# Layer norm of a convolution branch: mean and variance as four 32-column matmuls and one ones-product

## The reference, cut to what matters

```python
def layer_norm(x, gain, bias):
    xf = x.astype(jnp.float32)
    mu = jnp.mean(xf, axis=-1, keepdims=True)
    xc = xf - mu
    y = xc * lax.rsqrt(jnp.mean(xc * xc, axis=-1, keepdims=True) + EPS)
    ...
def conv_module(val, gate, dw_kernel, dw_bias, ln_gain, ln_bias):
    u = val * jax.nn.sigmoid(gate)
    u = lax.conv_general_dilated(u, ...)   # causal, depthwise, width 31
    u = layer_norm(u, ln_gain, ln_bias)    # over 512 channels
    return jax.nn.silu(u)
```

## Time and profile before

| | |
|---|---|
| median of three runs | 1696.66 us |
| span of the profiled execution | 1691.3 us |
| PE busy | 1543.5 us (91%) |
| DVE busy | 1233.8 us (73%) |
| ACT busy | 873.8 us (52%) |
| the four means and four variances, TensorE records of L521 and L528 | 64, of some 0.6 us each |

### The profile page before, as it was taken

One profiled execution on the slowest core, in us unless ns is written; L12 is line 12 of the kernel. 1 busy time (PEld: TensorE's weight loads), 2 busy tenths in 40 slices (PEclk: granted clock), 3 DMA queues, 4 the chain that ended last, 5 costly groups with the idle time before them and its releaser, 6 DMA issues. The chain is left out here.

```text
span 1691.3 us, 23716 instructions
## 1 busy us (share of the span) xinstructions
PE 1543.5 (91%) x7340; PEld 1130.4 (67%) x7342; DVE 1233.8 (73%) x1950; ACT 873.8 (52%) x1529; POOL 367.2 (22%) x395
## 2 busy tenths in 40 slices
PE   2699989999999999999999999847999999999974
PEld 2588846688956788855889766525667767677641
DVE  4589776479885498875497973486688778887737
ACT  2322363423384423474324263246688778887746
POOL 1000000100001000001000011014466667665640
PEclk9999998999999999999999999859999999999997
DMA  9342343233322333332332453169999998789959
GB/s 333 120 149 78 123 156 143 75 100 100 89 99 88 100 100 100 113 100 75 88 99 77 182 156 99 74 241 326 357 299 286 325 290 247 201 247 283 276 114 381
DMA packets 200420, 291.25 MB, mean 172 GB/s; under 512 B 10558, under 2 KB 158171, under 8 KB 200346
## 3 DMA queue, kind: packets, MB, share of 16 engines
q1 hardware_dynamic: 170720, 197.15, 34.0%
q0 software_dynamic: 29360, 92.99, 20.0%
q10 hardware_dynamic: 266, 0.14, 0.0%
HBM read 240.42 MB, written 59.26 MB: 177 GB/s over the span
## 5 line engine op out<-in xcount | busy, mean ns | idle before, releaser
L979 DVE SCALAR_TENSOR_TENSOR cv<-late_rows,taps,cv 128x512 f32<-128x512 f32 x480 | 321.7, 744 | 0.1
L1896 DVE TENSOR_TENSOR w_rest<-wgu,w_high 128x1024 fp32r<-128x1024 f32 x192 | 233.8, 1221 | 89.8 <-ACT w_high L1819 86.4
L1819 ACT ACTIVATE w_high<-wgu 128x1024 fp32r x192 | 201.7, 1054 | 97.0 <-PE pgu L1764 73.3
L497 PE MATMUL bank<-wo,yT 128*128 128x512 f32 x512 | 224.2, 594 | 3.6 <-ACT hT L683 2.5
L468 PE MATMUL bank<-hT_high,tiles_operand 128*128 128x512 f32 x512 | 204.3, 399 | 9.6 <-DVE hT_operand L952 8.5
L469 PE MATMUL bank<-hT_operand,tiles_operand 128*128 128x512 f32 x512 | 203.6, 398 | 0.0
L470 PE MATMUL bank<-hT_high,win_operand 128*128 128x512 f32 x512 | 203.6, 398 | 0.0
L497 PEld LDWEIGHTS bank<-wo,yT 128*128 128x128 f32 x512 | 95.7, 190 | 118.3 <-issue 116.3
L1774 PE MATMUL py<-wd,hTe 128*128 x384 | 172.7, 592 | 1.8 <-DVE hTe L1919 0.9
L1762 PE MATMUL pgu<-w_high,x_high 128*128 128x512 f32 x384 | 156.2, 407 | 3.8 <-DVE x_rest L1911 3.8
L1763 PE MATMUL pgu<-w_rest,x_high 128*128 128x512 f32 x384 | 151.4, 394 | 0.0
(11 more groups left out here) (369 smaller groups left out, 2824.9 us busy)
## 6 DMA issues: line engine op xcount, KB each, us to landing
win<-w_in_in SPq DMA_DIRECT2D x64, 512.0 KB, 5.0
wgu<-w_gate_in SPq DMA_DIRECT2D x32, 1024.0 KB
wgu<-w_up_in SPq DMA_DIRECT2D x32, 1024.0 KB
wd<-w_down_in SPq DMA_DIRECT2D x32, 1024.0 KB
win<-w_in_in SPq DMA_DIRECT2D x16, 1024.0 KB, 5.1
wo<-w_ada_in POOLq DMA_DIRECT2D x6, 2048.0 KB, 9.5
y_dram<-zeros POOLq DMA_DIRECT2D x17, 512.0 KB, 5.7
tiles<-x_in POOLq DMA_DIRECT2D x16, 512.0 KB, 6.1
```

Of the source, the lines that this page charges most:

```text
L497: last = nc.tensor.matmul(out[:], yT[:, w % 2, k, :], wo[:, k, half * 512:(half + 1) * 512], start=(k == 0), stop=(k == KD - 1))
L979: ins = V.scalar_tensor_tensor(out=cv[:, j], in0=u[:, j, w:w + T], scalar=tap, in1=cv[:, j], op0=ALU.mult, op1=ALU.add)
L1819: A(w_high[:, QK * q:QK * q + QK, :], c.wgu[:, bass.ds(slot, 1), QK * q:QK * q + QK, :].rearrange("p a k n -> p (a k) n"), ACT.Copy).then_ ...
L1896: V.tensor_tensor(w_rest[:, part, :], c.wgu[:, bass.ds(slot, 1), part, :].rearrange("p a k n -> p (a k) n"), w_high[:, part, :].bitcast(F3 ...
```

## The change

The mean is formed in two steps. Four matmuls, one for each slab, multiply 32 columns of ones (not 128) and write each its own 32 partitions of `pS`; they don't accumulate over each other. VectorE copies `pS` to SBUF (`save_mean`, into a slab of `sq` that is free), and one more matmul with the full ones (`whole_mean`) sums over the partitions. Since every sum then stands 32 times, the scale of the mean is divided by `GROUP` = 32 more. The variance is done alike, but ScalarE makes the copy (`save_variance`). Four semaphores are added. Where the entries stand in the lists is changed as well: "mean2" and "var2" are the second products, "msave" and "vsave" the copies.

```diff
             def mean(t):
                 pe.wait_ge(conv_step, (t + 1) * CONV_STEPS)
                 wait(pe, masked, t * NT)
                 for k in range(NCH):
-                    last = nc.tensor.matmul(pS[:], c.ones[:], cv[:, k, :], start=(k == 0), stop=(k == NCH - 1))
-                last.then_inc(mean_ready, 1)
+                    nc.tensor.matmul(pS[k * GROUP:(k + 1) * GROUP, :], c.ones[:, 0:GROUP], cv[:, k, :],
+                                     start=True, stop=True).then_inc(mean_parts, 1)
+
+            def whole_mean(t):
+                pe.wait_ge(mean_saved, t + 1)
+                nc.tensor.matmul(pS[:], c.ones[:], sq[:, NCH - 1, :], start=True, stop=True).then_inc(mean_ready, 1)
 
             def variance(t):
                 wait(pe, o_saved, t * NT)
                 for k in range(NCH):
                     pe.wait_ge(squared, t * NCH + k + 1)
-                    last = nc.tensor.matmul(pO[:], c.ones[:], sq[:, k, :], start=(k == 0), stop=(k == NCH - 1))
-                last.then_inc(var_ready, 1)
+                    nc.tensor.matmul(pO[k * GROUP:(k + 1) * GROUP, :], c.ones[:, 0:GROUP], sq[:, k, :],
+                                     start=True, stop=True).then_inc(var_parts, 1)
+
+            def whole_variance(t):
+                pe.wait_ge(var_saved, t + 1)
+                nc.tensor.matmul(pO[:], c.ones[:], sq[:, 1, :], start=True, stop=True).then_inc(var_ready, 1)
...
+            def save_variance(t):
+                act.wait_ge(var_parts, (t + 1) * NCH)
+                A(sq[:, 1, :], pO[:], ACT.Copy).then_inc(var_saved, 1)
...
+            def save_mean(t):
+                dve.wait_ge(mean_parts, (t + 1) * NCH)
+                V.tensor_copy(sq[:, NCH - 1, :], pS[:]).then_inc(mean_saved, 1)
```

The heads of the lists, before and after. TensorE:

```diff
-            FIRST = [("mean",), ("ada", 0), ("ada", 1), ("T", 0), ("var",), ("A", 0), ("T", 1), ("B", 0), ...
+            FIRST = [("mean",), ("ada", 0), ("mean2",), ("ada", 1), ("T", 0), ("var",), ("T", 1), ("var2",), ("A", 0), ("B", 0), ...
-            MIDDLE = [("y", 0, 0), ("T", 0), ("mean",), ("T", 1), ("y", 0, 1), ("T", 2), ("var",), ("T", 3), ("y", 1, 0),
+            MIDDLE = [("y", 0, 0), ("mean",), ("T", 0), ("mean2",), ("T", 1), ("y", 0, 1), ("T", 2), ("var",), ("T", 3), ("var2",),
-            FINAL = [("y", 0, 0), ("mean",), ("y", 0, 1), ("var",), ("y", 1, 0), ("y", 1, 1), ("A", 0), ...
+            FINAL = [("y", 0, 0), ("mean",), ("y", 0, 1), ("mean2",), ("y", 1, 0), ("var",), ("y", 1, 1), ("var2",), ("A", 0), ...
```

More of the change, by code:

```diff
@@ L613, in bias_rows @@
                 taken[3] = mod_ready, 3
-            FIRST = [("mean",), ("ada", 0), ("ada", 1), ("T", 0), ("var",), ("A", 0), ("T", 1), ("B", 0), ("O", 0), ("T", 2),
+            FIRST = [("mean",), ("ada", 0), ("mean2",), ("ada", 1), ("T", 0), ("var",), ("T", 1), ("var2",), ("A", 0), ("B", 0), ("O", 0), ("T", 2),
                      ("A", 1), ("columns",), ("B", 1), ("T", 3), ("O", 1), ("A", 2), ("oT", 0), ("B", 2), ("rows",),
@@ L624, in _ @@
                      ("r", 3), ("oT", 2), ("oT", 3), ("l", 3), ("piece", 1)]
-            FINAL = [("y", 0, 0), ("mean",), ("y", 0, 1), ("var",), ("y", 1, 0), ("y", 1, 1), ("A", 0), ("B", 0), ("O", 0),
+            FINAL = [("y", 0, 0), ("mean",), ("y", 0, 1), ("mean2",), ("y", 1, 0), ("var",), ("y", 1, 1), ("var2",), ("A", 0), ("B", 0), ("O", 0),
                      ("r", 0), ("A", 1), ("B", 1), ("l", 0), ("O", 1), ("A", 2), ("oT", 0), ("r", 1), ("B", 2),
@@ L643, in steps @@
                     else:
-                        {"y": y_half, "r": router_turn, "l": logits, "mean": mean, "var": variance, "A": scores, "B": state_sums,
+                        {"y": y_half, "r": router_turn, "l": logits, "mean": mean, "mean2": whole_mean, "var": variance, "var2": whole_variance, "A": scores, "B": state_sums,
                          "O": outputs, "oT": turn_outputs}[kind](t, *at)
@@ L865, in _ @@
                      ("raw", 1), ("sq", 0), ("sq", 1), ("sq", 2), ("xsum", 3), ("sq", 3), ("raw", 2), ("exps", 1),
-                     ("end", 1), ("raw", 3), ("ln", 3), ("exps", 2), ("end", 2), ("var",), ("ysum", 0), ("exps", 3),
+                     ("end", 1), ("vsave",), ("raw", 3), ("ln", 3), ("exps", 2), ("end", 2), ("var",), ("ysum", 0), ("exps", 3),
                      ("end", 3), ("gate",), ("key", 0), ("x1sum", 0), ("ysum", 1), ("key", 1), ("rin", 0), ("osq", 0),
@@ L872, in _ @@
             FINAL = [("ln", 0), ("ln", 1), ("ln", 2), ("end", 0), ("exps", 0), ("sq", 0), ("sq", 1), ("sq", 2), ("sq", 3),
-                     ("exps", 1), ("end", 1), ("ln", 3), ("exps", 2), ("end", 2), ("var",), ("ysum", 0), ("exps", 3),
+                     ("exps", 1), ("vsave",), ("end", 1), ("ln", 3), ("exps", 2), ("end", 2), ("var",), ("ysum", 0), ("exps", 3),
                      ("end", 3), ("gate",), ("key", 0), ("x1sum", 0), ("ysum", 1), ("key", 1), ("rin", 0), ("osq", 0),
@@ L888, in steps @@
                     else:
-                        {"ln": log_forget, "exps": head_exps, "end": end_exp, "sq": squares, "var": variance, "gate": conv_gate,
+                        {"ln": log_forget, "exps": head_exps, "end": end_exp, "sq": squares, "vsave": save_variance, "var": variance, "gate": conv_gate,
                          "ysum": y_sums, "x1sum": x1_sums, "rin": router_in, "key": save_keys, "osq": square_outputs,
@@ L1080, in centre @@
                 for k in range(NCH):
[L1081 removed]
+                    V.scalar_tensor_tensor(out=cv[:, k], in0=pS[:], scalar=-1.0 / (GROUP * DC), in1=cv[:, k],
                                            op0=ALU.mult, op1=ALU.add).then_inc(centred, 1)
@@ L1135, in gate_outputs @@
                 last.then_inc(o_gated, 1)
-            FIRST = [("scan", 0), ("scan", 1), ("diff", 0), ("centre",), ("head", 0), ("diff", 1), ("xnorm", 0), ("scan", 2),
+            FIRST = [("scan", 0), ("msave",), ("scan", 1), ("diff", 0), ("centre",), ("head", 0), ("diff", 1), ("xnorm", 0), ("scan", 2),
                      ("head", 1), ("diff", 2), ("scan", 3), ("xnorm", 1), ("head", 2), ("diff", 3), ("ada", 0),
@@ L1158, in _ @@
                      ("place", 3), ("rest", 1)]
-            FINAL = [("scan", 0), ("diff", 0), ("late", 0), ("centre",), ("head", 0), ("scan", 1), ("diff", 1), ("scan", 2),
+            FINAL = [("scan", 0), ("msave",), ("diff", 0), ("late", 0), ("centre",), ("head", 0), ("scan", 1), ("diff", 1), ("scan", 2),
                      ("head", 1), ("diff", 2), ("scan", 3), ("head", 2), ("diff", 3), ("scale",), ("head", 3),
@@ L1181, in steps @@
                     else:
-                        {"scan": scan, "diff": to_end, "head": decayed, "centre": centre, "scale": scale_conv, "mask": mask,
+                        {"scan": scan, "diff": to_end, "head": decayed, "msave": save_mean, "centre": centre, "scale": scale_conv, "mask": mask,
                          "state": next_state, "osave": save_outputs, "oms": output_squares, "gateo": gate_outputs, "place": place_conv,
```

9 lines of the change are left out of this document (5 added, 4 removed), and 2 rows, old and new, of the table MIDDLE.

## The result

| | before | after |
|---|---|---|
| median | 1695.61 us (1694.28 to 1696.83, 4 runs) | 1711.16 us (1706.75 to 1712.56, 4 runs) |
| ratio after/before | | 1.0084, 95% interval 1.0065 to 1.0103 |
| span of the profiled execution | 1691.3 us | 1709.9 us |
| mean granted clock of TensorE | 0.965 | 0.941 |

The account below looks back on a forecast made before the run. The prediction took no engine by itself as the bound, with three fixed-order lists close together. Its terms, 6.45 + 3.85 - 1.0 + 0.8 = +10.1 us, took the span from 1691.3 to 1701.4, plus 5.4 to the median: 1706.8 us, range 1700 to 1714.

Parts of the forecast that it names:

- The price of the parts (b): TensorE time for the four 32-column matmuls of one sum: 1.45 us, or 1.1 us with no stagger.
- Rival (a): Records start in program order, only neighbours overlap, so the four matmuls take 2.35 us: +14.6 us, 1711.3 us; chance 0.13.
- Rival (b): The four 32-column matmuls do not overlap and take 3.75 us: +21.6 us, 1718.3 us; chance 0.05.
- Block 3: In the last block var2 stands behind a half output projection, so ScalarE's queue and B 0 move later: +6.45 us.
- Block 0: In the first block mean2 stands behind "ada" 0, so VectorE's `centre` starts later and the delay goes through: +3.85 us.
- Blocks 1 and 2: In the middle blocks the load of tile 2 comes later but raw 3 sooner: -0.5 us each, -1.0 us together.
- The clock: In block 3 TensorE stands idle and drops to 1.2 GHz, slowing A 0 and O 0: +0.8 us, between nothing and 1.5.
- Rival (c): Delays of blocks 3 and 0 absorbed behind B 0: half leaves 1700.8 us, all leaves 1695.7 us; chance 0.12.
- Rival (d): TensorE's queue decides in all four blocks, late var2 and mean2 hold up nobody: 8.8 us less, 1687.9 us; chance 0.04.

Follow-up runs that it names:

- e12: e8 with the four 32-column products of each sum in blocks 1 and 2 all on the first 32 columns, accumulated; 1703.19 us, ratio 1.0047.
- e8: Kernel before with the new form and the change's own order in blocks 1 and 2 alone; 1692.40 us, ratio 0.9994.
- e1: Kernel before with the new form and new lists in block 3 alone; 1707.24 us, ratio 1.0064.
- e4: Kernel before with block 3's old variance matmuls moved behind both halves of the output projection, no 32-column tiles; 1710.26 us, ratio 1.0068.
- e11: Kernel before with the new form and the change's order in block 0 alone; 1695.46 us, ratio 1.0013.
- e7: Kernel before with the new form in blocks 1 and 2 alone, T 0 ahead of the mean and the mean's copy a step later; 1704.61 us, ratio 1.0044.
- e5: Changed kernel with unread 128x512 products filling TensorE's waits in block 3, seven ahead of A 0, four ahead of B 0; 1701.82 us, ratio 1.0037.
- e6: e2 with its 3.25 us wait ahead of B 0 of block 3 filled by four unread 128x512 products; 1702.15 us, ratio 1.0034.
- e10: e7 with some 1.3 us of unread products filling the wait ahead of B 0 of block 3; 1698.92 us, ratio 1.0013.
- e2: Changed kernel with block 3's variance parts right behind mean2 and var2 between the two halves of the output projection; 1707.41 us, ratio 1.0069.
- e9: Kernel before with some 1.3 us of unread products filling the wait ahead of B 0 of block 3; 1695.82 us, ratio 0.9999.

## Why the prediction was right or wrong

Forecast 1706.8 us in a range of 1700 to 1714, measured 1711.16: direction and range hold, the point is 4.4 us low. That it is no further off is in part luck: two errors of opposite sign stand in it, and the upper part of the range was there for program order, which didn't happen. By its steps:

- **The price of the parts (b).** Taken as 1.45 us with a lower bound of 1.1; measured 0.99 and 1.00 us in blocks 1 and 3 from the first record to the next work, and 1.15 us in block 3 with what the halves y around them take longer. The stagger was the wrong part: 0.4 us assumed, 0.02 us measured (473.31 to 473.33). The two switches of tile shape cost some 0.3 us together, not 0.2. Rival (a) gives 1711.3 us, nearly the measured time, and is wrong all the same: it needs b = 2.35. The time alone would have confirmed it; the rows at 473.31 and 474.30 do not. The Trainium skill, page "TensorE: Matmul & The Clock Gate", section "The mechanism" of Part 3, has matmuls start and end strictly in program order. Worked out for the order of records here, where the two of a slab are neighbours and share their columns, that was rival (a), and the trace disagrees with it: the first records of all four slabs start ahead of the second record of any, and the eight take 0.99 us. Rival (b), no overlap, falls with e12 beside e8.
- **Block 3.** Predicted +6.45 us; +6.0 us measured from the block's first projection to B 0. The shape holds in each part: Ln waits for var2 (4.52 us), ScalarE's queue behind it moves as a whole (10.76 us against 10.73), B 0 follows. The difference is b, which stands on the way to var2 twice, 0.3 us too high each time; the mean itself starts 0.1 us later in the block than before. e1 shows it alone, and e4 shows that the place in the list, not the new form, is the cause.
- **Block 0.** Predicted +3.85 us; +3.4 us, in the changed kernel and in e11, the difference again b. `centre` waits for mean2 as written. That B 0 passes the delay on is not what this block does: B 0 is only 1.6 us late, and 3.4 us arrive at the next projection all the same.
- **Blocks 1 and 2.** Predicted -0.5 us each, measured -0.87 each. The reason was right: the load of tile 2 is now what ScalarE waits for (0.69 us at 478.98), and y 1,0 follows raw 3. b being 0.45 us shorter there is enough for the difference of 0.37. e7, with T 0 first again, gets -1.2 us.
- **The clock: the step that failed in size.** I took +0.8 us with bounds 0 and 1.5, the price of A 0 and O 0 at the slow rows. I had foreseen the idle time (984 to 990.5 and to 995.7) and the lower level in it, but priced it only over the few records next to the wait. The row of 992 to 1020 us shows 0.66 over 28 us, and the product column above says that the whole stretch lengthens nearly in proportion, so that a us at half rate costs up to 0.5 us (an estimate from that column). +9.4 us between the profiled executions, 7.0 to 8.8 us in e1 to e4; e5 takes the idle time away and gets all of it back, e6 less than half. What the prediction lacked is thus a clock that is still low, and falls again, long after the wait has ended; for the second fall no cause is shown. With b = 1.0 and the other terms as measured, blocks 0 to 3 give 3.4 - 1.7 + 6.0 = +7.7 us; 15.5 us are measured, so about 8 are left for the clock; no run measures that rest by itself.
- **Rival (c), delays absorbed behind B 0.** Refuted for block 3: in e5, with the stretch at nearly the clock of the kernel before (0.96 and 0.94), 7.88 us at B 0 are 7.88 us at the last logits. In block 0 all 3.4 us reach the next projection. **Rival (d), TensorE's queue decides.** Only in blocks 1 and 2, and there 0.87 us arrive of the 2.8 that TensorE is freed of (twice 3.43 - 1.15 - 0.86).
- **The balance.** The terms other than the clock were 1.6 us too high together (9.3 against 7.7), nearly all of it through b; the clock was 7 us too low. The kernel before measured 1.05 us less than the median that the forecast started from, which leaves the 4.4 us.

The second product and the waits for it cost what the plan of the lists made them cost; taken alone the new form saves TensorE 3.43 - 1.15 - 0.86 = 1.4 us for each sum. No version here turns that into a gain that can be measured: the best, e8, is at 0.9994 (0.9972 to 1.0017).

## What to carry to other kernels

When a change puts a wait of several us on a TensorE-bound stretch, don't price only the wait and the records next to it: multiply the length of what follows by the drop in the mean granted clock that rows show after waits of that size, here some 8 us on top of 6. To know whether a loss behind a wait is the clock or the lateness, fill the wait with products that nobody reads and compare the same stretch again, slice by slice: a later fall of the clock may stay (e6, e10). Splitting one accumulated sum into parts and a second product needs two places in each engine's list; put the second one where its first reader's turn comes, not behind the next long entry (moving var2 forward in e2 brought B 0 3.6 us forward).

## What the runs showed of the hardware

- Four float32 products of 128x32 by 128x512 on four strips of columns: 1.00 us from the first to the next work; on one strip 3.55 us, 0.89 us for each product (e8, e12). On four strips the four first records start within 0.02 us, and with the switches of tile shape a group takes 1.15 us from a stream of 128-column products (after, block 3).
- Idle TensorE ahead of B 0 of block 3 of 2.1 us or more in the last wait (after, e1 to e4) came in all five traces with a clock that fell during the waits or within 3 us of B 0. With 1.4 to 1.6 us it fell there in two of five (e7 and e8, not in before, e11 and e12). With less than 0.5 us (e5, e6, e9, e10) in none of four. The Trainium skill, page "TensorE: Matmul & The Clock Gate", section "A second HAM failure mode: psum-queue depth-cycling", says that a matmul stream with many short idle times can swing between the two levels. That fits e7 and e8, where no single wait is long; but before, e11 and e12 have like waits and no fall there, and no run here takes the short waits apart one by one.
- A second fall, of 10 us, comes 63 to 69 us after B 0 in all traces with the first one (after, e1 to e4, e7, e8) and in e6 and e10, which have no first one. It is 3.4 us long in before, e11 and e12, and absent in e5 and e9. Its cause is open.
- The loss behind the wait does not grow with it: a last wait of 1.6 us (e7) and waits of 6.4 and 2.1 us (e4) both leave 115.4 us for the same stretch.
- The times of one kernel lie in two groups: 27 and 7 runs of the kernel before with medians some 7 us apart, 9 and 3 runs of e8 some 11 us apart. A median of few runs depends on how many fall in each, and a change of under 2 us, as in e8, disappears in that. That the clock makes the two groups is likely from the traces, but not shown.
